# A hybrid decoder trunk in fp32 on one core: query turns one slot later, accumulator freed one step earlier, the norm's factor folded into its epsilon, and 1 MB weight transfers in the second layer

## The reference

```python
def mla_layer(h, ...):                  # layer 0
    u = rms_norm(h, ln) @ w_in          # q latent 512 | kv latent 512 | rotary key 64 | gate 2048
    q = rms_norm(c_q, ln_q) @ w_q_up    # 16 heads x 192
    kv = rms_norm(c_kv, ln_kv) @ w_kv_up
    ... per-head norms of q and k, rotary part, causal softmax attention ...
    return h + (o * silu(gate)) @ w_o
k_sh, v_sh = shared_kv(h, ...)          # rms_norm(h) @ kv_w: 3 branches x 16 heads of k and v, k normed per head
def dilated_layer(h, k_sh, v_sh, ...):  # layer 1
    u = rms_norm(h, ln) @ w_in          # q of 3 branches x 16 heads | gate 2048
    ... per-head q norm, three dilated windows with ALiBi, merged by their denominators ...
    return h + (o * silu(gate)) @ w_o
def rms_norm(x, g): return x * rsqrt(mean(x*x) + EPS) * g
```

## Time and profile before

| what | value |
|---|---|
| time, median of 3 runs | 1463.5 us (1463.33 to 1464.04) |
| profiled execution, its own time | 1464.21 us |
| its span, first to last instruction | 1461.9 us |
| granted TensorE clock, mean | 0.998 |
| PE busy | 1440.6 us (99%) |
| DVE busy | 858.0 us (59%) |
| ACT busy | 690.3 us (47%) |
| POOL busy | 157.9 us (11%) |
| DMA, mean share of 16 engines over the span (main queue) | 52.0% |

### The profile page before, as it was taken

How to read it: one execution, slowest core, us unless ns; L and a number is a source line. 1 busy time by engine, 2 the same in 40 slices (tenths; PEclk the granted TensorE clock), 3 DMA queues, 4 the chain that set the end, 5 groups by cost and what they waited for, 6 DMA issues and landing times.

```text
span 1461.9 us, 22821 instructions
## 1 busy us (share of the span) xinstructions
PE 1440.6 (99%) x8008; PEld 1253.7 (86%) x8008; DVE 858.0 (59%) x1249; ACT 690.3 (47%) x988; POOL 157.9 (11%) x108
## 2 busy tenths in 40 slices
PE   8999999999999999999999999999999999999998
PEld 5799899999988888888888888888888888888998
DVE  7666776758955555555555655555554565545553
ACT  4555555544444445444445444544544444454432
POOL 5111111100011001010100200101010020011000
PEclk9999999999999999999999999999999999999999
DMA  8554444355556544654554554565555455456454
GB/s 310 167 159 133 142 136 140 136 176 177 183 198 193 193 148 163 199 168 154 192 176 145 187 190 145 171 199 162 158 187 188 144 174 192 152 173 193 154 167 136
DMA packets 70209, 250.61 MB, mean 171 GB/s; under 512 B 7792, under 2 KB 8176, under 8 KB 70000
## 3 DMA queue, kind: packets, MB, share of 16 engines
q1 hardware_dynamic: 69984, 248.38, 52.0%
q10 hardware_dynamic: 144, 1.05, 0.2%
HBM read 247.30 MB, written 2.10 MB: 171 GB/s over the span
## 4 chain that ended last, share of the span: by engine, by line
PE 94%; DVE 3%; DMA 1%; issue 1%; ACT 1%; POOL 0%; SPq 0%; DVEq 0%; ACTq 0%; POOLq 0%
PE acc L1102 84%; PE turn L1134 3%; PE pv_bank L1146 3%; PE score L1327 2%; DVE xa_lo L731 1%; PE score L1221 1%; PE score L1219 1%; PE turn L1205 0%; DMA res<-in_xT 0%; PE og_bank L1154 0%; DMA raw<-in_w_in 0%; DVE w_lo L716 0%; DVE xa_hi L728 0%; DVE gate L831 0%; ACT probT L497 0%
## 5 line engine op out<-in xcount | busy, mean ns | idle before, releaser
L716 DVE TENSOR_TENSOR w_lo<-raw,w_hi 128x1024 fp32r<-128x1024 f32 (+1 forms) x458 | 575.8, 1269 | 421.2 <-ACT w_hi L464 420.4
L464 ACT ACTIVATE w_hi<-raw 128x1024 fp32r<-128x1024 f32 x464 | 484.4, 1051 | 331.5 <-PE acc L1102 313.1
L1102 PE MATMUL acc<-w_hi,xa_hi 128*128 128x512 f32 (+1 forms) x1088 | 407.4, 374 | 7.2 <-POOL w_lo L385 4.9
L1102 PE MATMUL acc<-w_hi,xa_lo 128*128 128x512 f32 (+1 forms) x1088 | 398.2, 366 | 0.0
L1102 PE MATMUL acc<-w_lo,xa_hi 128*128 128x512 f32 (+1 forms) x1088 | 397.5, 365 | 0.0
L1102 PE MATMUL acc<-w_hi,xb_hi 128*128 128x512 f32 (+1 forms) x640 | 250.6, 392 | 2.7 <-DVE gate L835 1.8
L1102 PE MATMUL acc<-w_hi,xb_lo 128*128 128x512 f32 (+1 forms) x640 | 246.1, 385 | 0.0
L1102 PE MATMUL acc<-w_lo,xb_hi 128*128 128x512 f32 (+1 forms) x640 | 245.8, 384 | 0.0
L1102 PEld LDWEIGHTS acc<-w_hi,xa_hi 128*128 128x128 f32 x1088 | 205.9, 189 | 42.8 <-issue 10.0
L1102 PEld LDWEIGHTS acc<-w_hi,xa_lo 128*128 128x128 f32 x1088 | 205.6, 189 | 33.5
L1102 PEld LDWEIGHTS acc<-w_lo,xa_hi 128*128 128x128 f32 x1088 | 206.1, 189 | 30.7
(11 more groups left out here) (136 smaller groups left out, 1027.2 us busy)
## 6 DMA issues: line engine op xcount, KB each, us to landing
raw<-in_w_b SPq DMA_DIRECT2D x320, 512.0 KB, 3.4
raw<-in_w_gate SPq DMA_DIRECT2D x32, 512.0 KB, 3.4
raw<-in_w_out_a SPq DMA_DIRECT2D x32, 512.0 KB, 3.4
raw<-in_w_out_b SPq DMA_DIRECT2D x32, 512.0 KB, 3.6
raw<-in_w_kv SPq DMA_DIRECT2D x16, 512.0 KB, 3.5
raw<-in_w_in SPq DMA_DIRECT2D x15, 512.0 KB, 6.2
raw<-in_w_q SPq DMA_DIRECT2D x16, 384.0 KB, 3.0
out_T<-res SPq DMA_DIRECT2D x8, 256.0 KB, 4.1
```

The costliest lines, as they stand in the source:

```text
L464: nc.scalar.activation(w[0][:, s, 0:width], raw[:, s, 0:width], ACT.Copy).then_inc(hi_ready, 1)
L716: nc.vector.tensor_tensor(w[1][:, s, 0:width], raw[:, s, 0:width], w[0][:, s, 0:width].bitcast(F32), ALU.subtract).then_inc(lo_ready[0], 1)
L1102: last = nc.tensor.matmul(out, x(a), y(b), start=start and k == 0, stop=stop and k == 2, **more)
```

## The change

Five edits are made together.

1. `b_turn` of the first query block and ACT's copies of it move from slots 6 and 7 of a B pair to slots 7 and 8.
2. PE waits for `gate_step` in place of `gate_done` wherever it waits for a gate accumulator.
3. `r` leaves the chain of the input and B stages: ACT squares both tiles in one instruction without a scale, DVE adds EPS times (mean square of the token plus EPS) in place of EPS (a new small `x_eps`, computed once a layer), and POOL's power gives `rms` directly; its multiply by `r` is gone.
4. In the B stage SP loads steps 5 to 38 of a pair in 17 transfers of two steps (1 MB) each, into two neighbouring slots; it waits for `lows` of the second step's slot. Steps 0 to 4 and 39 stay single.
5. ACT waits for the semaphore of the transfer that brings its step (`raw_of`).

```diff
+        def raw_of(n, static_n):
+            slot = static_n % RING
...
+            if s < RING:
+                return raw_full[slot], i + (earlier + 1)
+            if s == RING:
+                return raw_fifth_full, i + 1
+            if s == B_STEPS - 1:
+                return raw_last_full, i + 1
+            two = (s - RING - 1) // 2
+            return raw_two_full[two % 2], i * (9 - two % 2) + (two // 2 + 1)
...
-                for s in range(B_STEPS):
-                    load((i, B_STEPS), B_0 + s, w_b[i, s], STEP)
+                for s in [*range(RING + 1), *range(RING + 1, B_STEPS - 1, 2), B_STEPS - 1]:
+                    slot, count = (B_0 + s) % RING, 2 if RING < s < B_STEPS - 1 else 1
+                    signal, value = low_of((i, B_STEPS), B_0 + s + count - 1 - RING)
+                    sp.wait_ge(signal, value)
+                    full, _ = raw_of((i, B_STEPS), B_0 + s)
+                    sp.dma_start(raw[:, slot:slot + count], w_b[i, s:s + count].rearrange("s p k -> p s k"))\
+                        .then_inc(full, 16)
...
-                nc.gpsimd.tensor_tensor(root[:, 0:width], ms[:, 0:width], mhalf[:, 0:width], ALU.pow)\
-                    .then_inc(pool_step, 1)
-                pool.wait_ge(pool_step, c + 1 if times_r == "in" else c - (B_CHAIN_0 - 3))
-                u = width // TILES
-                nc.gpsimd.tensor_tensor(rms[:, 0:width].rearrange("p (t u) -> p t u", t=TILES),
...
-                                        ALU.mult).then_inc(rms_ready, 1)
+                nc.gpsimd.tensor_tensor(rms[:, 0:width], ms[:, 0:width], mhalf[:, 0:width], ALU.pow)\
+                    .then_inc(rms_ready, 1)
...
-                if by_tile:
-                    for t in range(TILES):
-                        last = nc.scalar.activation(rows[:, buf, t, 0:width], acc[:, pair, t, 0:width], ACT.Square,
-                                                    scale=r[:, t:t + 1])
-                else:
-                    last = nc.scalar.activation(rows[:, buf, :, 0:width], acc[:, pair, :, 0:width], ACT.Square)
-                last.then_inc(squares, 1)
+                nc.scalar.activation(rows[:, buf, :, 0:width], acc[:, pair, :, 0:width], ACT.Square)\
+                    .then_inc(squares, 1)
...
-                    if s in (6, 7):
-                        g = s - 6
+                    if s in (7, 8):
+                        g = s - 7
                         turned(b_round(i, 5 + g), qT[:, g * 512:g * 512 + 512], 512, q_gain[:, g:g + 1])
...
-                nc.vector.tensor_scalar(ms[:, 0:n], ss[:, 0, 0:n], 1.0 / span, EPS, ALU.mult, ALU.add)\
-                    .then_inc(means, 1)
+                dve.wait_ge(x_scaled, g + 1)
+                nc.vector.scalar_tensor_tensor(
...
+                    op0=ALU.mult, op1=ALU.add).then_inc(means, 1)
...
                         if later:
-                            pe.wait_ge(gate_done, i)
+                            pe.wait_ge(gate_step, i)
...
-                    if s in (6, 7):
-                        b_turn(i, 0, b_round(i, s - 1), 2 * (s - 6))
+                    if s in (7, 8):
+                        b_turn(i, 0, b_round(i, s - 2), 2 * (s - 7))
```

More of the change, by code:

```diff
@@ L178, in build_program @@
         ms = sb("ms", [P, 8])
-        root = sb("root", [P, 8])
         rms = sb("rms", [P, 8])
         x_ms = sb("x_ms", [P, TILES])
+        x_eps = sb("x_eps", [P, TILES])
         tok_ss = sb("tok_ss", [P, 2 * TILES])
@@ L248, in build_program @@
         raw_full = [sem(f"raw_full{s}") for s in range(RING)]
+        raw_fifth_full = sem("raw_fifth_full")
+        raw_last_full = sem("raw_last_full")
+        raw_two_full = [sem(f"raw_two_full{s}") for s in range(2)]
         hi_ready = sem("hi_ready")
@@ L307, in step_count @@
             return n if isinstance(n, int) else n[0] * n[1] + static_n
+        def raw_of(n, static_n):
+            slot = static_n % RING
+            if static_n < B_0:
+                if isinstance(n, int):
+                    return raw_full[slot], n // RING + 1
+                return raw_full[slot], n[0] * (n[1] // RING) + (static_n // RING + 1)
+            earlier = (B_0 - 1 - slot) // RING + 1
+            if isinstance(n, int) and n >= OUT_B_0:
+                return raw_full[slot], earlier + PAIRS + (n - OUT_B_0) // RING + 1
+            i, s = divmod(n - B_0, B_STEPS) if isinstance(n, int) else (n[0], static_n - B_0)
+            if s >= B_STEPS:
+                return raw_full[slot], i + (earlier + 2)
+            if s < RING:
[6 more added lines that the diff above has]
+            return raw_two_full[two % 2], i * (9 - two % 2) + (two // 2 + 1)
         def low_of(n, static_n):
@@ L413, in _ @@
                     stream_rms(0)
-                    chain(0, TILES, "in")
+                    chain(0, TILES)
                 if n == 15:
-                    chain(1, TILES, "in")
+                    chain(1, TILES)
                 if n + 4 < LOW_0 and n % 2:
@@ L434, in b_pair @@
                         if s == at:
-                            chain(i * 4 + (B_CHAIN_0 + k), units * TILES, "b")
+                            chain(i * 4 + (B_CHAIN_0 + k), units * TILES)
                     if attend and s == 13:
@@ L670, in b_pair @@
                         n, pair = b_fill(i, par, K01)
-                        chain_squares(i * 4 + (B_CHAIN_0 + 1), 1, n, pair, 512, True)
+                        chain_squares(i * 4 + (B_CHAIN_0 + 1), 1, n, pair, 512)
                     if s in (9, 10):
@@ L676, in b_pair @@
                         n, pair = b_fill(i, par, K2V0)
-                        chain_squares(i * 4 + (B_CHAIN_0 + 2), 0, n, pair, 256, True)
+                        chain_squares(i * 4 + (B_CHAIN_0 + 2), 0, n, pair, 256)
                         for t in range(TILES):
@@ L774, in stream_mean, with chain_sums @@
                 last.then_inc(x_mean, 1)
-            def chain_sums(c, buf, units, span):
+                for t in range(TILES):
+                    last = nc.vector.tensor_scalar(x_eps[:, t:t + 1], x_sum[t], EPS / D, EPS * EPS, ALU.mult, ALU.add)
+                last.then_inc(x_scaled, 1)
+            def chain_sums(c, buf, units, span, g):
                 dve.wait_ge(squares, c + 1)
```

50 lines of the change are left out of this document (23 added, 27 removed).

## The result

The changed kernel takes 1455.79 us (median of 5 runs, 1454.49 to 1457.01); the kernel before took 1463.6 us on the same chip (5 runs, 1463.33 to 1466.39). The ratio is 0.9942, with a 95% interval of 0.9928 to 0.9956: 7.8 us less. The forecast was 1456.2 us. The profiled execution's span went from 1461.9 to 1454.0 us.

A forecast was written before the change was run, and what follows sets the result against it. PE was taken as the bound, busy 1440.6 of 1461.9 us. Gains of 5.95 + 0.5 + 0.85 + 0 = 7.3 us off 1464.2 gave 1456.9, and a median 0.7 lower gave 1456.2; range 1452 to 1460.

The forecast's parts named there:

- The turns, 5.95 us: Slot 6 of seven B pairs: PE's wait for ACT's `probT` goes, 0.85 us each; bounds 0 and 6.1.
- The rivals that took half or all of it back: B pairs, slots 7 to 13: hidden wait takes back half (1459.8 us, chance 0.10) or all (1462.1, chance 0.08).
- The gate, 0.5 us and not 3.7: MLA pair boundaries: eight waits of 0.46 us vanish, but six only move to slot 2; bounds 0 and 3.7.
- The exact sign that had been named: MLA slot 2: matmul still 0.13 us after L953, wait of about 0.5 us named, period same to 0.05 us.
- the rival's size: MLA stage: a looser dependency chain makes the gate's gain real, 3.2 us more, 1453.0 us; chance 0.12.
- The 0.1 and 0.4 us: Gate's gains: 0.1 us at the second MLA pair, 0.4 at the last wait, ahead of the output projection.
- The norm's factor, 0.85 us: Input stage: 0.43 us ahead of POOL's `w_lo` and 0.43 at the latents' second chain; bounds 0.5 and 1.2.
- The 1 MB transfers, 0: B stage: PE waits for no transfer, so no gain; later landing stays hidden by steps made ahead.
- the deciding point of 7.3 us: B stage: landing beyond which 1 MB transfers bound it, 48 us per microsecond; slower rival, chance 0.07.
- The loop's re-entry: Between B pairs: fetching instructions beside larger transfers may take 1 or 2 us longer, 1458 us; chance 0.03.
- the ring: MLA stage: 16.5 us through DVE, ACT and POOL by turns to L953, then PE; sets the pair's period.

The follow-up runs named there:

- e8_three: Changed kernel with three `w_lo` of an MLA pair (slots 7, 0 and 1) made later on DVE: 1450.67 us, ratio 0.991.
- e2_gate: Kernel before with only PE waiting for `gate_step` in place of `gate_done`: 1463.27 us, ratio 0.9998.
- e3_chain: Kernel before with only `r` folded into the epsilon (one square instruction, no multiply on POOL): 1462.43 us, ratio 0.9994.
- e1_turns: Kernel before with only the query turns of a B pair moved to slots 7 and 8: 1457.3 us, ratio 0.996.
- e7_late: Changed kernel with each 1 MB transfer waiting for the `w_lo` of one step more before it is issued: 1617.12 us, ratio 1.1046.
- e5_defer: Changed kernel with slot 7's `w_lo` of an MLA pair made behind the next pair's query rows and rotation: 1457.31 us, ratio 0.9955.
- e9_three_done: `e8_three` with PE's waits for the gate put back to `gate_done`: 1453.88 us, ratio 0.9932.

## Why the prediction was right, point by point

The forecast of 1456.2 us missed by 0.4, inside its range.

- **The turns, 5.95 us: right.** Alone they gave 6.3 us (median), 0.2 above the upper bound of 6.1 but within its scatter, and no wait took their place. The six periods of the gate in the B stage shrank by 5.4 us, of which 6 x 0.85 make 5.1; the other 0.3 is about what loop re-entries moved (below). The rivals that took half or all of it back are out. What was said of ACT held: the first query copy, with ACT idle 0.60 us ahead of it, costs nobody anything.
- **The gate, 0.5 us and not 3.7: right, and for the reason given.** Alone the median fell by 0.3 us, with an interval that includes none. The exact sign that had been named, a wait of about half a microsecond at L953's successor with an unchanged period, is in the trace: 0.57 us and 199.0 against 199.1. It also holds from the other side: with the rings shortened, the gate's wait is worth 3.2 us. That was the rival's size, for a kernel that this one was not. Two small readings were off and changed nothing. PE can start the next matmul 0.18 us after the first of the two transposes (201.85 to 202.03 in the kernel after), not 0.22. And it can start 0.02 to 0.03 us after the output turn (`e8_three`), not 0.11, so it came 0.3 us too early to slot 2, not 0.22. The 0.1 and 0.4 us that make up the 0.5 can't be told apart in the medians.
- **The norm's factor, 0.85 us: right in its parts, a little more in sum.** Ahead of POOL's `w_lo` the multiply saved 0.28 us (0.24 said). The squares went from 1.25 us to 1.01 us in one instruction, by ACT's timeline of the kernel after at 40.10 (0.19 said, 0.24 measured), together 0.52. At the latents' turn PE starts 0.51 us sooner after its last matmul (0.43 said). By these rows it is 1.0 us, inside the bounds of 0.5 to 1.2. Whole starts can't confirm it: the start of L974 in the first pair moved up by 1.4 us from before to after, but in `e2_gate`, which has no edit ahead of it, it moved up by 1.0 as well. So single profiles of different programs differ by about a microsecond in the input stage. For the same reason the sign that POOL's `w_lo` would be waited for 0.4 us less can't be read from the lists, which give 3.3 to 4.9 us without edit 3 and 2.7 to 4.1 in `e3_chain` and the kernel after. The median of `e3_chain` says 1.2 us, with an interval from 0.4 us slower to 2.2 us faster.
- **The 1 MB transfers, 0: right.** Landing was put at 5.1 us, between 5.1 and 6.8; it was 4.9, a little below the lower bound, since the second 512 KB added 1.5 us (4.9 against 3.4) where 1.7 had been taken from the rate of the page's first slice. ACT's longest wait was put at some 2 us and was 2.5. The median landing did not come near the deciding point of 7.3 us. By the page "DMA: Bandwidth & Descriptors" of the Trainium skill, section "Bandwidth", a transfer of 1 MB takes 6.15 us when GpSimd issues it. Those that SyncE issues here took 4.9 us, and the measurement decides.
- **The loop's re-entry: small, and to the other side.** The prediction gave a rival 1 to 2 us of loss there. Such places cost 0.9 us once before and 0.8 us in three places after, none above 0.4; the total did not grow. That also accounts for the turns' other 0.3 us: in the window of the B stage PE stopped so for 0.9 us before, 0.5 after and 0.3 in `e1_turns`.

What the prediction did not see is how near a second chain lies. It called the ring "the whole period of a pair". Shortening only that ring made the pairs longer, through the key rows, and it took two more moved instructions to get at the 4.5 us that lay in the stage. By the median of `e8_three` the kernel before had at least 13.2 us to give (1463.86, its median in that run, to 1450.67), of which this change took 7.8.

## What to carry to other kernels

Before you count a removed wait as a gain, go on to the next place where the same engine meets the same partners; if it already comes too early there, the wait only moves. The distance between the first and the last start of one repeated line settles it better than the list of waits does, since the list did not even name the wait that mattered.

When a ring of several engines sets a period, look for the next ring before you shorten the first: what is put off on a busy engine lands in front of another chain. Test an edit that seems worth nothing again once the ring is gone, since here the same edit went from about nothing (0.3 us, not told from 0) to 3.2 us.

A merged transfer that is hidden gains nothing and uses up slack. Work out the turn-round (landing, copies, hand-overs) against the steps it must fit into. When you test it by a delay, ask what else the delay changes: in `e7_late` one `w_lo` more left one transfer under way at a time, and halved the time for the turn-round.

## What the runs showed of the hardware

- A small power on POOL (128x4) took 1.01 us in `e5_defer` with no large DVE instruction beside it, and 1.94 us before beside a DVE subtraction of 128x1024 with both inputs in SBUF; that subtraction was not slowed. In the B stage it is DVE that loses: a `w_lo` took 4.26 us beside a POOL multiply of 4.42 us. The row of POOL's timeline of the kernel after, and then that of DVE's:

```profile
943.01 4.42 POOL L462 TENSOR_TENSOR phase<-phase,half 128x2048 f32<-128x2048 f32 x1
```

```profile
944.26 4.26 DVE L729 TENSOR_TENSOR w_lo<-raw,w_hi 128x1024 fp32r<-128x1024 f32 x1 [0.28 <-ACT w_hi L482]
```

  The Trainium skill, "SBUF — State Buffer", section "Who interferes with whom", says that a DVE instruction with two SBUF inputs contends with a GpSimd instruction that reads SBUF; the trace agrees, 1.94 us against 1.01 and 4.26 us against 1.23. In both places the instruction that started second is the one that took longer: the power started at 207.34, 0.15 us after the `w_lo` beside it, and this `w_lo` at 944.26, 1.25 us after the multiply; it ended 1.09 us after the multiply did. The multiply was itself started 0.26 us after another `w_lo` (942.75), and its seven executions took 4.42 us where they took 3.6 before.
- From the end of a DVE instruction to the start of the PE matmul that waits for it 0.13 to 0.14 us pass, for the gate as for the query rows.
- PE stops where a loop is entered again, with no releaser shown: 0.2 to 0.9 us in the kernels before and after, 2.1 and 2.2 us in the B stage of `e7_late`. A wait at the same place can cover it, as the gate's does in `e9_three_done`. What PE does in that time the traces do not show.
